# A hybrid decoder layer with 32 experts: one weight place freed at the merge, two chunks given back in halves, a transpose behind a down chunk

## The reference, cut to what matters

```
x  = x + W_out( sigmoid(G_a) * P_a(HGRN2(x')) + sigmoid(G_b) * P_b(RWKV7(x')) )   # x' = RMSNorm(x)
x2 = RMSNorm(x) * norm2_w
logits = x2 @ router_w + router_b ;  top 4 of 32 experts, gates = softmax of the 4 logits
per expert: h = rows @ w_gu[e] + b_gu[e]         # w_gu[e]: 1024 x 2048, 8 MB
            act = clamped SwiGLU(h)
            out = act @ w_down[e] + b_down[e]    # w_down[e]: 1024 x 1024, 4 MB
x  = x + sum of gate * out ;  y = RMSNorm(x)
```

## Time and profile before

| what | value |
|---|---|
| median of three runs | 1319.65 us (1319.37 to 1320.62) |
| the profiled execution | 1320.38 us, of it the profile's span 1318.7 us |
| PE busy | 1286.6 us, 98% of the span |
| DVE, ACT, POOL busy | 28%, 18%, 4% |
| TensorE's granted clock | 0.999 of full speed |
| HBM read | 443.82 MB, 340 GB/s over the span |

### The profile page before, as it was taken

How to read it: one execution, slowest core, us unless ns; L and a number is a source line. 1 busy time by engine, 2 the same in 40 slices (tenths; PEclk the granted TensorE clock), 3 DMA queues, 4 the chain that set the end, 5 groups by cost and what they waited for, 6 DMA issues and landing times.

```text
span 1318.7 us, 18430 instructions
## 1 busy us (share of the span) xinstructions
PE 1286.6 (98%) x7369; PEld 615.0 (47%) x7369; DVE 373.0 (28%) x1017; ACT 241.9 (18%) x532; POOL 52.9 (4%) x129
## 2 busy tenths in 40 slices
PE   9999999999999999999999999999999999999997
PEld 6778778888744333333333333333333323233333
DVE  3234756554317121121211212112112111211112
ACT  3143343222122110111101111011101101110102
POOL 5000200000060000000000000000000000000000
PEclk9999999999999999999999999999999999999999
DMA  7635437101869999999999999999999999999996
GB/s 234 173 98 191 136 82 272 33 33 34 323 197 415 429 429 428 429 429 429 417 428 429 430 429 430 429 430 429 430 430 429 429 430 430 429 430 429 428 428 260
DMA packets 72736, 449.40 MB, mean 341 GB/s; under 512 B 14404, under 2 KB 43126, under 8 KB 47880
## 3 DMA queue, kind: packets, MB, share of 16 engines
q1 hardware_dynamic: 67090, 445.72, 82.6%
q10 hardware_dynamic: 5590, 2.88, 0.7%
HBM read 443.82 MB, written 4.76 MB: 340 GB/s over the span
## 4 chain that ended last, share of the span: by engine, by line
PE 78%; DMA 17%; DVE 2%; ACT 1%; issue 0%; SPq 0%; DVEq 0%; ACTq 0%
PE bank L1260 25%; PE bank L1280 13%; DMA ring<-in_expert_w_gu_dram 7%; PE bank L561 7%; PE bank L651 5%; PE bank L1168 5%; DMA arena<-in_expert_w_gu_dram 5%; PE bank L1199 4%; DMA extra<-in_expert_w_down_dram 3%; PE bank L1075 2%; DMA extra<-in_expert_w_gu_dram 2%; PE bank L1049 2%; PE bank L942 2%; ACT arena L1407 1%; PE bank L1175 1%; PE bank L925 1%
## 5 line engine op out<-in xcount | busy, mean ns | idle before, releaser
L1260 PE MATMUL bank<-arena 128*64 128x512 f32 x960 | 216.6, 594 | 1.0 <-DMA arena<-in_expert_w_gu_dram 1.0
L1407 ACT ACTIVATE arena<-bank 128x512 f32<-128x512 f32 (+6 forms) x232 | 115.2, 515 | 485.4 <-PE bank L1280 196.3
L1260 PE MATMUL bank<-ring,arena 128*64 128x512 f32 x848 | 189.7, 594 | 3.9 <-DMA ring<-in_expert_w_gu_dram 3.9
L1407 ACT ACTIVATE arena<-arena 128x256 f32<-128x256 f32 (+7 forms) x124 | 68.9, 564 | 469.6 <-DVE arena L2355 462.5
L2355 DVE TENSOR_SCALAR arena<-bank 128x256 f32<-128x256 f32 x64 | 27.0, 421 | 377.9 <-PE bank L1260 377.9
L1260 PEld LDWEIGHTS bank<-arena 128*64 128x64 f32 x960 | 67.2, 137 | 134.4 <-issue 116.9
L1260 PEld LDWEIGHTS bank<-ring,arena 128*64 128x64 f32 x848 | 59.5, 137 | 116.1 <-issue 100.2
L2405 DVE COPY arena<-bank 64x512 f32<-64x512 f32 x30 | 20.8, 694 | 319.7 <-PE bank L1280 319.7
L1280 PE MATMUL bank<-arena 128*64 128x512 f32 x448 | 100.6, 595 | 0.3 <-DMA arena<-in_expert_w_down_dram 0.3
L1280 PE MATMUL bank<-ring,arena 128*64 128x512 f32 x448 | 99.8, 595 | 0.0
L1168 PE MATMUL bank<-arena 128*64 128x512 f32 x372 | 89.6, 599 | 0.0
(11 more groups left out here) (372 smaller groups left out, 1127.0 us busy)
## 6 DMA issues: line engine op xcount, KB each, us to landing
arena<-in_expert_w_gu_dram SPq DMA_DIRECT2D x60, 2048.0 KB, 24.2
ring<-in_expert_w_gu_dram SPq DMA_DIRECT2D x53, 2048.0 KB, 21.8
arena<-in_expert_w_down_dram SPq DMA_DIRECT2D x28, 2048.0 KB, 27.4
ring<-in_expert_w_down_dram SPq DMA_DIRECT2D x28, 2048.0 KB, 21.6
extra<-in_expert_w_gu_dram SPq DMA_DIRECT2D x15, 2048.0 KB, 24.2
ring<-in_w_in_dram SPq DMA_DIRECT2D x23, 1024.0 KB, 5.4
extra<-in_expert_w_down_dram SPq DMA_DIRECT2D x7, 2048.0 KB, 32.3
ring<-in_w_out_dram SPq DMA_DIRECT2D x4, 1024.0 KB, 7.5
```

What stands on the lines that cost most here:

```text
L1260: ins = mm(bank[q % 2][64 * (q // 2):64 * (q // 2) + 64, :], gu_lhs(c), w[:, q * 512:(q + 1) * 512], start=(c == 0), stop=(c == KT - 1), s ...
L1407: return nc.scalar.activation(out, in_, f, **kw)
```

## The change

norm2_w goes to fm[9] instead of norm_bc, and is loaded behind `merged` 8, where fm[9] comes free, instead of ahead of chunks 0 and 4. The copy of the sample rows goes to x2[:, 2] instead of fm[0], the squares to `qk`, the router's weights to another part of tm, `fold` to `inb`. So nothing is left in place 9 after the merge, and chunk 9 is issued there, behind chunk 5, instead of last.

Two chunks are given back in halves: PE counts w_used also after the first half (8 of 16 matmuls) of chunk 0 and of chunk 4, which is expert 0's first down chunk. SP loads chunks 11 and 15 as two DMAs of 1 MB each. PE waits for the first halves too (`half_loaded`). All counts of w_used behind these go up by two.

PE's order changes: `weights_T` stands behind the second gate/up chunk instead of the first, and in every pair `pick_T` stands behind the first down chunk instead of ahead of it. The last pair's second half (pe_last) keeps its order.

```diff
@@ places and counts
-        res2 = fm[0][:, 0:D]
+        norm2_bc = fm[9][:, 0:D]
-        rw_sb = arena[:, off_par:off_par + KT * NE]
+        rw_sb = tm[:, 1728:1728 + KT * NE]
-        fold = arena[:, off_par + NT:off_par + NT + NE]
+        fold, sq_n = inb[:, 0:NE], qk[:, 0:512]
+        HALVED = (0, 4)
+        USED = len(HALVED)
+        def used(i, n):
+            return n + sum(h < n for h in HALVED) if isinstance(i, int) and i == 0 else i * (2 * ECH) + (USED + n)
@@ SP
-            sp.dma_start(norm_bc, norm2_w.partition_broadcast(P)).then_inc(S("norm_loaded"), 16)
             w_load(sp, 0, 0)
             w_load(sp, 0, 4)
             sp.wait_ge(S("merged"), 8)
+            sp.dma_start(norm2_bc, norm2_w.partition_broadcast(P)).then_inc(S("norm_loaded"), 16)
             for x in (0, 2, 3):
                 sp.dma_start(braw[NE * x:NE * x + NE, :], expert_b_gu[0]).then_inc(S("braw_loaded"), 16)
             w_load(sp, 0, 5)
+            w_load(sp, 1, 9)
             sp.wait_ge(S("x_added"), 1)
...
             sp.wait_ge(S("logits"), 2)
             w_load(sp, 1, 8)
-            sp.wait_ge(S("xn_done"), 7)
-            sp.wait_ge(S("rstd"), 6)
-            w_load(sp, 1, 9)
             for n in range(FULL, PEELED + QUAD * ECH):
-                sp.wait_ge(w_used, before_chunk(n) + 1)
-                w_load(sp, n // ECH, n)
+                b = before_chunk(n)
+                if b in HALVED:
+                    sp.wait_ge(w_used, used(0, b + 1) - 1)
+                    w_load(sp, n // ECH, n, None, 0)
+                sp.wait_ge(w_used, used(0, b + 1))
+                w_load(sp, n // ECH, n, None, 1 if b in HALVED else None)
@@ PE, gate_up
+                    if isinstance(quad, int) and quad == 0 and s0 + c / 2 == FULL + HALVED[1]:
+                        pe.wait_ge(S("half_loaded"), 32)
-                    if first and c == 2:
+                    if first and c == 4:
                         weights_T()
-                    if c % 2 == 1:
+                    if c % 2 == 1 or (first and c == 0):
                         ins.then_inc(w_used, 1)
@@ PE, down
-                ins.then_inc(w_used, 1)
+                    if r == 3 or (r == 1 and isinstance(quad, int) and quad * (QUAD * ECH) + s in HALVED):
+                        ins.then_inc(w_used, 1)
@@ PE, pe_pair
-                    pe.wait_ge(S("xg_evac"), i * 2 + x + 2)
-                    pick_T()
-
                     pe.wait_ge(S("actT_evac"), i * 2 + x + 1)
                     for j in range(DN):
+                        if static and quad == 0 and s0 + GU + j == FULL + HALVED[0]:
+                            pe.wait_ge(S("half_loaded"), 16)
                         down(quad, s0 + GU + j, j, bank[1], dn_lhs)
+                        if j == 0:
+                            pe.wait_ge(S("xg_evac"), i * 2 + x + 2)
+                            pick_T()
@@ ACT, residual_norm; DVE, norm_rows and last_rows
-                        i = fn(res2[r, c], out, ACT.Copy)
+                        i = fn(x2[r, 2, c], out, ACT.Copy)
-                                                   in1=norm_bc[0:rows, c], op0=ALU.mult, op1=ALU.mult)
+                                                   in1=norm2_bc[0:rows, c], op0=ALU.mult, op1=ALU.mult)
```

More of the change, by code:

```diff
@@ L480, in _ @@
                     for s in range(j * ECH, (j + 1) * ECH):
-                        sp.wait_ge(w_used, quad * (QUAD * ECH) + (s - WS + 1))
+                        sp.wait_ge(w_used, quad * (QUAD * ECH) + (USED + s - WS + 1))
                         w_load(sp, e, PEELED + s)
@@ L485, in _ @@
                 for s in range(j * ECH, (j + 1) * ECH):
-                    sp.wait_ge(w_used, last * (QUAD * ECH) + (s - WS + 1))
+                    sp.wait_ge(w_used, last * (QUAD * ECH) + (USED + s - WS + 1))
                     w_load(sp, e, PEELED + s)
@@ L1362, in pe_last @@
                         late_down(0, r, b, c)
-                pe.wait_ge(S("half_loaded"), 16)
+                pe.wait_ge(S("half_loaded"), 16 * (len(HALVED) + 1))
                 for r in range(2):
@@ L1728, in residual_norm @@
                     for out, c in acc(t):
-                        i = fn(res2[r, c], out, ACT.Copy)
+                        i = fn(x2[r, 2, c], out, ACT.Copy)
                     done_wait(act, i, "act_step")
-                    halves = [res2[r, h * 512:(h + 1) * 512] for h in range(2)]
+                    halves = [x2[r, 2, h * 512:(h + 1) * 512] for h in range(2)]
                 for h in range(2):
@@ L1736, in residual_norm @@
                         act.wait_ge(S("xn_done"), 6 + h)
-                    done_wait(act, fn(sq2[r, h * 512:(h + 1) * 512], halves[h], ACT.Square, accum_out=st3[r, 2 * t + h:2 * t + h + 1]),
+                    done_wait(act, fn(sq_n[r, :], halves[h], ACT.Square, accum_out=st3[r, 2 * t + h:2 * t + h + 1]),
                               "act_step")
@@ L1803, in act_pair @@
                     fn(xT, bank[6][:, :], ACT.Copy).then_inc(S("rows_evac"), 1)
-                    act.wait_ge(w_used, i * (2 * ECH) + ECH * (x + 1))
+                    act.wait_ge(w_used, used(i, ECH * (x + 1)))
                     fn(yo[64 * x:64 * x + 64, 0:512], bank[1][0:64, :], ACT.Copy).then_inc(S("y_evac"), 1)
@@ L1832, in _ @@
             fn(xT, bank[0][:, :], ACT.Copy).then_inc(S("actT_evac"), 1)
-            act.wait_ge(w_used, last * (2 * ECH) + (2 * ECH - DN))
+            act.wait_ge(w_used, last * (2 * ECH) + (USED + 2 * ECH - DN))
             fn(yo[0:64, 0:512], bank[6][0:64, :], ACT.Copy).then_inc(S("y_evac"), 1)
@@ L2223, in norm_rows @@
                     dve.wait_ge(S("rstd"), 3 * n + x + 1)
-                    for out, c in acc(t) if t < 2 else [(res2[0:rows, 0:512], slice(0, 512)), (res2[0:rows, 512:D], slice(512, D))]:
+                    for out, c in acc(t) if t < 2 else [(x2[0:rows, 2, 0:512], slice(0, 512)), (x2[0:rows, 2, 512:D], slice(512, D))]:
                         i = v.scalar_tensor_tensor(out=dst[0:rows, t, c], in0=out, scalar=st3[0:rows, 12 + t:13 + t],
-                                                   in1=norm_bc[0:rows, c], op0=ALU.mult, op1=ALU.mult)
+                                                   in1=norm2_bc[0:rows, c], op0=ALU.mult, op1=ALU.mult)
                     step(i, "xn_done")
@@ L2247, in last_rows @@
                     dve.wait_ge(S("wo_done"), 4)
-                step(v.tensor_tensor(x2[:, 1, c], out, norm_bc[:, c], ALU.mult), "xn_done")
+                step(v.tensor_tensor(x2[:, 1, c], out, norm2_bc[:, c], ALU.mult), "xn_done")
             last_rows(0)
@@ L2402, in dve_pair @@
                     next_rows(i, x)
-                    act_rows(i, x, i * LOOP_STEPS + 5 * x + 2, i * (2 * ECH) + (ECH * x + GU))
-                    dve.wait_ge(w_used, i * (2 * ECH) + ECH * (x + 1))
+                    act_rows(i, x, i * LOOP_STEPS + 5 * x + 2, used(i, ECH * x + GU))
+                    dve.wait_ge(w_used, used(i, ECH * (x + 1)))
                     v.tensor_copy(yo[64 * x:64 * x + 64, 512:1024], bank[1][64:128, :]).then_inc(S("y_evac"), 1)
@@ L2413, in _ @@
             next_rows(last, 0)
-            act_rows(last, 0, last * LOOP_STEPS + 2, last * (2 * ECH) + GU)
+            act_rows(last, 0, last * LOOP_STEPS + 2, last * (2 * ECH) + (USED + GU))
             dve.wait_ge(S("act_ready"), last * 2 + 1)
             dve.wait_ge(S("actT"), last * 2 + 1)
-            act_rows(last, 1, last * LOOP_STEPS + 6, last * (2 * ECH) + 2 * GU)
-            dve.wait_ge(w_used, last * (2 * ECH) + (2 * ECH - DN))
+            act_rows(last, 1, last * LOOP_STEPS + 6, last * (2 * ECH) + (USED + 2 * GU))
+            dve.wait_ge(w_used, last * (2 * ECH) + (USED + 2 * ECH - DN))
             done(v.tensor_copy(yo[0:64, 512:1024], bank[6][64:128, :]), "xn_done")
```

## The result

The changed kernel takes 1322.88 us (median of 11 runs, 1322.0 to 1323.79) against 1319.9 us of the kernel before (11 runs, 1319.37 to 1320.75): ratio 1.0022, 95% interval 1.0014 to 1.003. It is slower by 3.0 us. The forecast was 1320.4 with a range to 1322.6. The profiled execution took 1323.79 us, its span is 1322.0 us, 3.3 us over that of before.

The account below looks back on a forecast made before the run. The prediction took the stream of weights as the bound: a 3.7 us lead, used up at chunk 60 by PE's later releases, leaves +0.4 us, 1320.8 from the profiled execution; with medians up to 0.7 lower, 1320.4, range 1317.0 to 1322.6.

Parts of the forecast that it names:

- The stream sets the end: Whole kernel: the stream of weights at 430 GB/s, not PE, sets the end; six 2 MB chunks take 29.3 us.
- The sum at chunk 60: At expert 8's down: release 2.1 us later, landing at 664.3 instead of 663.9, so +0.4 us to the end.
- part 2: Start of the experts: of 4.9 us offered, the stream runs 3.7 us ahead from 443 us, with halves and weights_T moved.
- Part 3: pick_T behind the first down chunk: PE 0.53 us later per x = 1 expert and expert 0, later x = 0 free.
- The 7.7 us: A 2 MB chunk issued into idle queues lands 7.7 us later: 4.9 transfer and 2.8 fixed.
- the second scarce chunk: Sign of being wrong: a second hole, at a chunk not reckoned as scarce, would break the sum on the slow side.
- Part 1: At the merge: chunk 9 issued near 365.5, over near 388 ahead of chunk 6, takes 4.88 us out of the stream.
- Part 4: norm2_w loaded behind the merge: lands at 373, costs nothing if it lands before about 376.3.
- Rival (c): norm2_w comes late; from 376.3 each us adds one to the total, 1324.1 at a landing of 380; chance 0.11.
- The skill's rules: Transfer is about 2.0 us plus bytes over 436 GB/s, 6.8 for 2 MB (not used); ring order, used for norm2_w.
- The chances: Whole kernel, against 0.2% (2.6 us): faster 0.16, same 0.72, slower 0.12; the forecast itself 0.68.

Follow-up runs that it names:

- e2: The kernel before with only pick_T moved behind the first down chunk: 1322.9 us, ratio 1.0026.
- e1: The changed kernel with pick_T ahead of the first down chunk again, the rest as changed: 1318.71 us, ratio 0.9995 against the kernel before.
- e7: e3 without the halves and with weights_T back in its old place: 1319.9 us, ratio 1.0 against the kernel before.
- e3: e1 with three quads written out instead of two: 1319.39 us, ratio 0.9995 against the kernel before.
- e5: The kernel before with three quads written out instead of two, nothing else: 1320.32 us, ratio 1.0003.

## Why the prediction was wrong

- **The stream sets the end.** Right. All twelve kernels keep 428 to 430 GB/s from 800 us to 1280, and what differs is lost ahead of that.
- **The sum at chunk 60: the step that failed for the time.** The place was right, two terms were too small. PE's lateness was forecast at 2.1 us and is 3.5; the landing was forecast at 7.7 us from the issue and took 8.7. Forecast: issue 2.1 us later, landing at 664.3. Measured: issue 4.1 us later (3.5 from PE, 0.5 from the later start), landing at 667.2, against 663.9 before. These 3.3 us are those of the two spans. The lead of part 2 doesn't enter the forecast of the time, since the sum has it used up at chunk 60 in any case.
- **Part 3, pick_T: why PE was later.** Mechanism right, size wrong. Down waits for ACT, pick_T filled that wait, and moved it costs: forecast 0.53 us in expert 0 and the x = 1 experts, nothing in the x = 0 ones. Measured, from act_T to the first work of the next expert: 0.72 to 0.74 in experts 0, 1, 5 and 7; 0.15 in expert 3, where b_down fills the wait; 0.30 in 2, 4, 6 and 8. The 0.2 to 0.3 that I left out is, as far as the starts tell, the same in both kinds: the two down chunks are cut apart by the transposes, and behind each change of shape PE goes on about 0.1 us later than within a run.
- **The 7.7 us.** It was read from chunks 2 and 6. In the twelve traces 20 whole chunks from chunk 6 on were issued late enough that the issue and not the queue should set their landing. In 14 of them, twelve of which are chunk 6 itself, no packet of the kind that the profile calls "instruction" (16 KB, 0.9 to 1.1 us on one engine) starts between issue and landing, and they land after 7.5 to 7.8 us. In the other six one does, and they take 8.7 to 9.4. Chunk 60 of the changed kernel is of the second kind, and that of e2 of the first; there chunk 61 has the packet, and lands 7.05 us behind chunk 60 instead of 4.9. No run moved such a packet, so that it is the cause is a reading of the traces and not shown. The DMA queues from chunk 60's issue to its landing, in the changed kernel (658.53:667.2, 8.7 us) and in e2 (657.75:665.32, 7.6 us); packets, MB, share:

```profile
q1 hardware_dynamic: 184, 2.70, 83.3%
q8 instruction: 1, 0.02, 0.6%
...
q1 hardware_dynamic: 174, 2.46, 89.7%
```

- **Chunk 56.** The prediction doesn't reckon it. Issued at 636.9 on dry engines, it has another hole ahead of it (233 GB/s in 632:640, 3.7 us). By the prediction's own numbers its issue would have moved from 632.4 to 635.1 and its landing to 642.8, behind the 640.6 of a stream that is 3.7 us ahead: the second scarce chunk could have been seen. It would only have used up lead that chunk 60 takes as well.
- **Part 1, chunk 9 in the gap.** Right: issued at 366.1, landed at 388.3, chunk 6 undisturbed.
- **Part 2, a lead of 3.7 us.** Wrong, though it doesn't change the forecast of the time. The rule behind it was that a chunk lands 7.7 us after its issue or 4.9 after the one before, whichever is later. Chunk 12 was forecast at 424.0, 3.9 ahead, and landed at 416.7 + 9.2 = 425.9, 2.0 ahead; it is one of the six with an "instruction" packet. By chunk 18 the lead was 1.1 us (456.2 against 457.3), 1.6 without the later start; in e1, which starts the same way, it was 2.4 at this chunk. The rule looks at the landing alone, which is that of the last of 16 engines. Chunk 8 landed at 413.1, yet already from 411 to 412 only 66 GB/s moved: most engines had run dry some 2 us before the landing. What the stream loses is the idle time of these, and a chunk that arrives in time for the last engine is late for the others. The GB/s show this for all engines together; the views don't tell the engines apart. By the windows the start lost 3.9 us more than in the kernel before (7.9 against 4.0 in 392:440). e7 and e3 show it without anything behind: -2.6 and -3.7 us were due by the rule, 0.0 and -0.4 came (-0.4 and -0.9 against e5).
- **Part 4, norm2_w.** Right. It landed at about 374 (forecast 373), DVE waited 10.3 us, and add_x of tile 0 came when it had before. e1 has nearly the same wait (9.4 us) and is no slower than the kernel before. Rival (c) did not happen.
- **The skill's rules.** The Trainium skill's "DMA: Bandwidth & Descriptors" (section "Anatomy of one DMA") gives the fixed 2.0 us for DMAs that GpSimd issues; the prediction applied it to loads that SP issues and didn't say so. The estimate from it would have had chunk 60 land 6.8 us from its issue; the trace has 8.7, farther off than my 7.7. The same page's "Queues, rings and completion order" in the Trainium skill says that a copy is split over up to 16 rings, one for each engine, and that each engine takes its own ring's descriptors in order. That is what part 2 needed: the trace agrees, by the 66 GB/s in 411:412 ahead of a landing at 413.1. I used the section for norm2_w alone.
- **The chances.** 0.72 for "within 0.2%" and 0.12 for slower rested on a sum whose errors nearly all point one way: each unmodelled break, "instruction" packet or dry engine only adds, and only expert 3 cost less than reckoned. The range missed the median by 0.3 us, but its centre missed it by 2.5.

## What to carry to other kernels

A stream of loads over many engines is not one server: measure what a late issue costs by the GB/s in narrow windows ahead of it, not by the spacing of landings, and expect much of what a transfer gains in an early gap to be lost again at the next release that can't be made earlier. Before an instruction is moved out of a place where its engine waits anyhow, look for what will stand in that wait afterwards; here 0.5 us per expert were free in the old place. Take a load's time to landing from examples at several places of the kernel: here the same 2 MB took 7.5 to 9.4 us. A bound engine's slack is not even along the kernel: find where the buffer count or the order of places changes, since that is where another engine's lateness comes through.

## What the runs showed of the hardware

- Four transposes of 128 x 128 cost PE 0.53 us in the middle of matmuls (650.24 to 650.77 in the kernel before), and cutting a run of matmuls in two with them costs about 0.1 us more at each side: chunk 52 takes 3.58 us from its start to that of pick_T, where the two down chunks in one run took 7.02 us, 3.51 each (650.77 to 657.79 in the kernel before).
- A 2 MB load whose landing was set by its issue landed after 7.5 to 7.8 us where no packet of the profile's kind "instruction" fell between issue and landing (14 loads, twelve of them chunk 6), and after 8.7 to 9.4 us where one did (six loads). The first halves of chunk 11, 1 MB each, landed after 4.9 to 5.2 us, none with such a packet.
- Loads of 2 MB land 4.9 us apart in a full queue, but now and then one is late, by up to 1.7 us (6.4 instead of 4.9 at 610 and 1280 us in the kernel before). In the twelve traces 48 landings in a full queue came more than 0.2 us late; at 47 of them an "instruction" packet lies between 5 us before the landing ahead and their own, which is so for a fifth of all landings (447 of 2189). In the kernel before the two packets start at 607.6 and 1277.2 us. The landings behind a late one follow at 4.9 us again, and the windows around 610 us lose only about 0.2 us of bytes (426 GB/s in 600:620).
